# Two transformer blocks on one Trainium2 core: selected-keys attention on key partitions, and norms in two halves of tokens

## The reference

```python
# block 1
h = rms_norm(x, g_mix)
q, k, v, qi, ki, wi, conv_in, qc, gate_pre = split(h @ w_in)
y_att  = dsa_attention(rope(q), rope(k), v, rope(qi), rope(ki), wi) @ w_att_out
y_conv = (bg * causal_dwconv(cg * u)) @ w_conv_out
y_mem  = memory_attention(qc, rms_norm(mem, g_mem) @ w_mem_kv) @ w_mem_out
x = x + (sigmoid(gates) * [y_att, y_conv, y_mem]).sum() @ w_o
gate, val = split(causal_dwconv(rms_norm(x, g_ffn) @ w_up))
x = rms_norm(x + (silu(gate) * val) @ w_down, g_final)
# block 2: stick-breaking attention (12 heads) and memory attention (4 heads)
y = concat(stick_breaking(x @ w_in_sb), memory_attention_2(x, mem_2 @ w_mem_kv_2)) @ w_out
x = layer_norm(x + y)
x = layer_norm(x + square(relu(x @ w_up_2)) @ w_down_2)
# dsa_attention, for each block of 128 queries: 6 heads of 64, 2 groups of keys/values
score = sum_h(wi * relu(qi @ ki.T)), causal
sel = top_k(score, 256)
p = softmax(q @ k[sel].T / 8)      # three heads share a group's keys
o = p @ v[sel]
```

## Time and profile before

| | us |
|---|---|
| median of 3 runs (lowest to highest) | 3177.89 (3175.38 to 3183.56) |
| the profiled execution, its own time | 3180.83 |
| its span | 3179.0 |
| mean granted TensorE clock, share of full speed | 0.957 |

### The profile page before, as it was taken

How to read it: one execution, slowest core, us unless ns; L and a number is a source line. 1 busy time by engine, 2 the same in 40 slices (tenths; PEclk the granted TensorE clock), 3 DMA queues, 4 the chain that set the end, 5 groups by cost and what they waited for, 6 DMA issues and landing times.

```text
span 3179.0 us, 35178 instructions
## 1 busy us (share of the span) xinstructions
PE 2945.3 (93%) x13338; PEld 2381.2 (75%) x13338; DVE 1697.7 (53%) x2259; ACT 755.1 (24%) x1320; POOL 1168.0 (37%) x649
## 2 busy tenths in 40 slices
PE   5977999998999899999999779999888999999996
PEld 3765878885778688888888567887676888888885
DVE  4475899985562533232332547888937333333327
ACT  3154000003531211011111245666613000000002
POOL 2320334441024233433444414555532443334331
PEclk9978999996999899999999889999988999999998
DMA  3110112221031011111112110000020111111111
...
DMA packets 42300, 165.39 MB, mean 52 GB/s; under 512 B 4688, under 2 KB 5968, under 8 KB 40656
## 3 DMA queue, kind: packets, MB, share of 16 engines
q1 hardware_dynamic: 35568, 129.31, 12.1%
...
...
## 4 chain that ended last, share of the span: by engine, by line
PE 81%; DVE 10%; issue 5%; ACT 2%; POOL 1%; DVEq 1%; DMA 1%; ACTq 0%; SPq 0%; POOLq 0%
PE dense L457 22%; PE dense L458 21%; PE dense L461 21%; DVE stay L1654 2%; PE dense L799 2%; PE side L708 2%; PE dense L800 2%; PE dense L801 2%; PE dense L718 1%; PE dense L635 1%; PE side L837 1%; DVE a_lo L1319 1%; DVE T L1263 1%; ACT T L977 1%; PE side L497 1%
## 5 line engine op out<-in xcount | busy, mean ns | idle before, releaser
L366 POOL TENSOR_TENSOR w_hi<-raw,zero 128x1024 fp32r<-128x1024 f32 x210 | 404.6, 1926 | 1586.7 <-PE dense L461 1475.4
L457 PE MATMUL dense<-a_hi,w_hi 128*128 128x512 f32 x2192 | 864.9, 395 | 42.4 <-DVE a_lo L1319 20.0
L458 PE MATMUL dense<-a_lo,w_hi 128*128 128x512 f32 x2192 | 860.7, 393 | 0.0
L461 PE MATMUL dense<-a_hi,w_lo 128*128 128x512 f32 x2192 | 681.1, 392 | 0.0
L368 POOL TENSOR_TENSOR w_lo<-raw,w_hi 128x1024 fp32r<-128x1024 f32 x210 | 530.6, 2527 | 16.5
L457 PEld LDWEIGHTS dense<-a_hi,w_hi 128*128 128x128 f32 x2192 | 416.2, 190 | 140.2 <-issue 40.2
L458 PEld LDWEIGHTS dense<-a_lo,w_hi 128*128 128x128 f32 x2192 | 416.1, 190 | 87.6 <-issue 1.2
L461 PEld LDWEIGHTS dense<-a_hi,w_lo 128*128 128x128 f32 x2192 | 415.6, 190 | 87.9
L457 PE MATMUL dense<-b_hi,w_hi 128*128 128x512 f32 x864 | 338.8, 392 | 5.4 <-DVE T L1567 2.5
L458 PE MATMUL dense<-b_lo,w_hi 128*128 128x512 f32 x864 | 336.3, 389 | 0.0
L1547 DVE TENSOR_TENSOR x_res<-x_res,dense 128x1024 f32<-128x1024 f32 x104 | 126.9, 1220 | 332.8 <-PE dense L461 331.1
...
## 6 DMA issues: line engine op xcount, KB each, us to landing
...
x_in<-in_x_t SPq DMA_DIRECT2D x4, 1024.0 KB, 8.7
...
```

Of the source, the lines that this page charges most:

```text
L366: pool.tensor_tensor(w_hi[:, r % 2, :], raw[:, r, :], zero[:, 0:1].broadcast_to([P, D]), ALU.add).then_inc(weights_rounded, 1)
L457: pe.matmul(o, w_hi[:, slot, w], hi[:, k, x], start=b == 0, stop=False)
L458: pe.matmul(o, w_hi[:, slot, w], lo[:, k, x], start=False, stop=False)
L461: last = pe.matmul(o, w_lo[:, slot, w], hi[:, k, x], start=False, stop=stop)
```

## The change

**Attention.** Keys lie on partitions. A step is (block i, group g) with the group's three heads side by side (384 columns): 16 steps, and 72 pieces (step, block of 128 keys). A piece is four fp32r matmuls into one bank (keys by rounded queries, keys by the queries' rest, mask by three identities, a row of ones by the row of negative bounds), an exponential of 128x384 on ACT, and one fp32 matmul with `v_ones`: 64 columns of values and 64 of ones, so that the output has the row sums beside the values. The bound is the row's masked maximum of logits made in one fp32r matmul, still with queries on partitions (`bound_logits`), in 48 maxima on DVE as before; three one-row matmuls turn the negated bounds (`turn_bounds`) and ACT copies them. At a step's end DVE takes the reciprocal of the 64x384 row sums and multiplies. `k_stack` (key and its rest) and `v_ones` are made ahead of the convolution stage; per step ACT rounds the queries twice (64x384) and DVE takes the rests. POOL makes the mask in six pieces. The bounds of step s stand on PE between the pieces of steps s-2 and s-1.

**Norms.** The 1024 tokens go in two halves of 512. Norm 0 loads x by halves and sums its squares with 8 fp32 matmuls a half, without DVE additions. For norms 1 and 3 the last two tiles before are done by halves (`last_two`: half 0 of both, then half 1 with the sums and the spread of half 0 between), and the first two tiles behind likewise (`first_two`: half 0 of both, the second tile four slices behind, with the second half's sums ahead of slice 2 and its spread ahead of slice 6). Norm 4 has its last four down outputs by halves and 16 stores. KV2's four tiles move from before REST to behind the last down tile, and norm 2's sums and spreads stand between them. The two first `w_o` tiles lose their lag of four slices (`two_tiles` had the second tile four slices behind the first).

```diff
-T_KV2 = T_FF + FULL * FF_TILES
-T_REST = T_KV2 + 4
-T_MEM2 = T_REST + 2 * REST + KB // 2
+T_REST = T_FF + FULL * FF_TILES
+T_KV2 = T_REST + 2 * REST + KB // 2
+T_MEM2 = T_KV2 + 4
...
+DSA_LEAD, DSA_LAG = 3, 2
+
+
+def bound_at(s, j):
+
+    first, last = DSA_X0[s - 2] - 1, DSA_X0[s - 1] - 2
+    return first + (last - first) * j // (REP - 1)
...
+NORM_SPLIT = (None, 2, 0, 2, 4)
+
+
+def pieces(norm):
+
+    m = NORM_SPLIT[norm]
+    return [(k, None) for k in range(KB - m)] + [(k, h) for h in range(2) for k in range(KB - m, KB)]
...
+            for h in range(2):
+                for c in range(4):
+                    sp.dma_start(x_in[:, 2 * c:2 * c + 2, cols(h)], io["x_t"][:, 2 * c:2 * c + 2, cols(h)]
+                                 ).then_inc(x_loaded[h][c], 16)
+                sp.dma_start(raw[:, h, :], io["w_stream"][h]).then_inc(weights_loaded[h], 16)
...
+            pool.wait_ge(picked, 1)
+            for i in range(TOPK // P, TB):
+                sc = slice(score_at(i), score_at(i + 1))
+                pool.tensor_scalar(mask_r[:, sc], score[:, sc], TAKEN / 2, NEG, ALU.is_gt, ALU.mult).then_inc(masked, 1)
...
+            def first_two(t, u, ready, sums=None, spread=None, sums_at=2, spread_at=6, lag=4):
+
+                for n in range(KB + lag):
+                    if n == sums_at and sums is not None:
+                        sums()
+                    if n == spread_at and spread is not None:
+                        spread()
...
+            def square_sums(norm, h):
+
+                pe.wait_ge(added, added_before(norm, KB - 2, h) + 1)
+                sum_part(T[:, 3, :], cols(h), 0, True, False)
+                pe.wait_ge(squares, squares_before(norm, KB - 1, h) + 1)
+                sum_part(T[:, (KB - 1) % 2, :], cols(h), 0, False, True).then_inc(sum_ready, 1)
...
+            def last_two(norm, t, u, sums):
+
+                for m in range(2):
+                    pe.wait_ge(sums_free[(u + m) % 2], (u + m) // 2)
+                    pe.wait_ge(weights_split, t + m + 1)
+                    half_product(t + m, half_bank(norm, KB - 2 + m, 0), a_hi, a_lo, 0, 0, KB, KB).then_inc(half_tile, 1)
+                o = half_bank(norm, KB - 2, 1)
+                half_product(t, o, a_hi, a_lo, 1, 0, 3, KB)
+                sums(0)
+                half_product(t, o, a_hi, a_lo, 1, 3, KB, KB).then_inc(tile_done, 1)
+                spread(norm, 0)
+                half_product(t + 1, half_bank(norm, KB - 1, 1), a_hi, a_lo, 1, 0, KB, KB).then_inc(tile_done, 1)
...
+            def bound_logits(n):
+
+                s, j = n // REP, n % REP
+                i, g = DSA_PLAN[s]
+                pe.wait_ge(dup_split, s + 1)
                 if n >= 2:
-                    b = n - 2
-                    i = DSA_PLAN[b][0]
-                    pe.wait_ge(lg_tc, TB + b + 1)
...
+                o = att_logit_bank(x)
+                pe.matmul(o, k_stack[:, g, keys], qd_hi[:, s % 4, :, :], start=True, stop=False)
+                pe.matmul(o, k_stack[:, g, keys], qd_lo[:, s % 4, :, :], start=False, stop=False)
+                pe.matmul(o, mask_r[:, score_at(i) + kb * P:score_at(i) + kb * P + P], ident3[:, :, :], start=False, stop=False)
+                pe.matmul(o, one_row[:, :], bound_row[:, s % 2, :], start=False, stop=True).then_inc(d_logits, 1)
...
+                pe.matmul(att_out_bank(s), v_ones[g][:, kb, :], att_w[:, x % 4, :], start=kb == 0, stop=kb == i
+                          ).then_inc(d_out, 1)
...
+            for x in range(len(DSA_KEYS) + DSA_LAG):
+                if x < len(DSA_KEYS):
+                    att_logits(x)
+                if x + 1 in DSA_X0[DSA_LEAD - 1:DSA_STEPS - 1]:
+                    turn_bounds(DSA_X0.index(x + 1) + 1)
+                for n in BOUND_AT.get(x, ()):
+                    bound_logits(n)
+                if x >= DSA_LAG:
+                    att_values(x - DSA_LAG)
...
             for n in range(4):
+                if n == 1:
+                    for h in range(2):
+                        square_sums(2, h)
+                if n == 3:
+                    for h in range(2):
+                        spread(2, h)
                 tile(T_KV2 + n, U_KV2 + n, hi=m_hi, lo=m_lo, width=MEM, ready=parts["mem2"][1] if n == 0 else None)
...
+            for g in range(GROUPS):
+                act.activation(k_stack[group_rows(g), g, :], k_f[group_rows(g), :], ACT.Copy).then_inc(kv_round, 1)
+            for g in range(GROUPS):
+                act.activation(v_ones[g][:, :, 0:HD], v_f[:, :, HD * g:HD * g + HD], ACT.Copy)
+                act.activation(v_ones[g][:, :, HD:P], v_f[:, :, HD * g:HD * g + HD], ACT.Copy, bias=1.0, scale=0.0)
...
+                    act.activation(att_w[:, x % 4, :], att_logit_bank(x), ACT.Exp, scale=SCALE).then_inc(d_exp, 1)
...
-                dve.tensor_tensor_reduce(out=T[:, n % 2, 0:w], in0=side[:, n % 2, 0:w],
-                                         in1=score[:, score_at(i):score_at(i) + w], scale=1.0, scalar=TAKEN, op0=ALU.add,
-                                         op1=ALU.max, accum_out=row_max[:, e:e + 1])
-                dve.drain()
-                dve.tensor_scalar(neg_max[:, e:e + 1], row_max[:, e:e + 1], -SCALE, None, ALU.mult).then_inc(lg_max, 1)
-                dve.wait_ge(lg_exp, TB + n + 1)
-                dve.reciprocal(inv_sum[:, e:e + 1], row_sum[:, e:e + 1])
-                dve.drain()
-                dve.tensor_scalar(T[:, n % 2, 0:w], T[:, n % 2, 0:w], inv_sum[:, e:e + 1], None, ALU.mult
-                                  ).then_inc(lg_p, 1)
...
+                dve.tensor_tensor_reduce(out=masked_out[:, n % 2, 0:w], in0=side[:, n % 2, 0:w],
+                                         in1=mask_r[:, score_at(i):score_at(i) + w].bitcast(F32), scale=1.0, scalar=TAKEN, op0=ALU.add,
+                                         op1=ALU.max, accum_out=row_max[:, e:e + 1]).then_inc(d_max, 1)
+                if n % REP == REP - 1:
+                    e -= REP - 1
+                    dve.drain()
+                    if s >= 2:
+                        dve.wait_ge(d_row, s - 1)
+                    dve.tensor_scalar(neg_max[:, e:e + REP], row_max[:, e:e + REP], -1.0, None, ALU.mult).then_inc(d_neg, 1)
...
+                    dve.wait_ge(d_out, e + 1)
+                    dve.reciprocal(att_inv[:, s % 2, :], att_out_bank(s)[HD:P, :])
+                    dve.drain()
+                    dve.tensor_tensor(ya_f[group_rows(g), :, i * P:i * P + P],
+                                      att_out_bank(s)[0:HD, :].rearrange("p (j q) -> p j q", j=REP),
+                                      att_inv[:, s % 2, :].rearrange("p (j q) -> p j q", j=REP), ALU.mult).then_inc(d_copied, 1)
...
```

931 lines of the change are left out of this document (630 added, 301 removed).

## The result

The changed kernel takes 3188.58 us (median of 8 runs, 3181.84 to 3195.77) against 3178.71 (8 runs); the ratio is 1.0031, with a 95% interval of 1.0018 to 1.0044. It is slower by 0.3%, where 3114 was forecast with a range of 3082 to 3148. The profiled execution has a span of 3180.8 us. It took 3182.97, 5.6 under the median of its eight: three of them (3181.84 to 3183.31) have a mean granted clock of 0.962 to 0.964, the other five (3188.38 to 3195.77) of 0.958 to 0.961, so a difference of medians to the changed kernel and one of traces need not agree.

What follows compares the result with a forecast made beforehand. TensorE, busy 93% of the span, was taken as the bound, so gains come from its waits or less or cheaper work: 12 + 9 + 2 + 16.5 + 15 + 5.5 + 3 = 63 us off 3180.8, 3114 in medians, range 3082 to 3148.

Steps and rivals of the forecast that it cites:

- A piece is four fp32r matmuls at 0.23 us or less: Attention on PE: each of a piece's four 384-column fp32r matmuls costs 0.23 us or less, about 0.175 at full clock.
- That is 1.35 to 1.5 a piece: Attention on PE: four fp32r matmuls plus one fp32 PV take 1.35 to 1.5 us a piece, 97 to 108 in all.
- The uncovered tail: End of attention: the last reciprocal, product, rounding and POOL's low part stay uncovered, 5.7 us where 2.17 was.
- Rival C: Attention: low clock or DVE stays last, 0 to +15 us instead of -12; 3126 to 3141, typically 3136; chance 0.18.
- rival E: Attention: the reciprocal chains the stage, from about 9.5 us an instruction; slower, 3186 or more; chance 0.03.
- Rival D: Norms 0, 1, 3, 4: POOL meetings and doubled instructions leave 10 us gain instead of 34; 3138 to 3158; chance 0.08.
- the fixed part of the doubled instructions: Norms: fixed cost of doubled DVE instructions eats gain; a 512 operation costs 0.62 of pace, half of 1.16 is 0.58.
- Norm 0: Start of kernel: first product near 24.5 instead of 48.5, two tiles end near 63 instead of 72.4; -9 us (5 to 11).
- The merged tiles without lag: -2: First w_o tiles behind the attention: dropping the lag saves 2 us (0 to 3).
- Norm 1: Behind w_o: from tile 7's first half, end at 42 to 43.5 us instead of 59.6; -16.5 (13 to 20).
- I counted two: Two-input DVE operations meeting POOL cost 2.2 us each; one more in norms 0, 1, 3, attention each gives back 9.
- Norm 2, 3, 4: Later norms: norm 2 with KV2 takes 23 us, -15 (10 to 17); norm 3 -5.5 (3 to 9); norm 4 -3 (0 to 6).

Runs made afterwards that it cites:

- e1: Changed kernel with the attention of before put back, all else (halved norms) still changed: 3168.89 us, ratio 0.9969 to the kernel before.
- e2: Changed kernel with the bound added by a matmul over 128 rows, 127 of them zero, instead of one row: 3164.99 us, ratio 0.9954 to the kernel before.
- e13: Changed kernel with the bound's matmul over 64 rows, 63 of them zero, instead of one: 3181.06 us (one run).
- e14: Changed kernel with the bound's matmul over 32 rows instead of one: 3186.29 us (one run).
- e11: Changed kernel with 128-row bound matmul, w_o lag put back, second memory's low part moved behind the feed-forward groups, wide diagonals: 3133.55 us, ratio 0.9861 to kernel before.
- e10: Changed kernel with old attention, w_o lag put back, second memory's low part moved behind the feed-forward groups, wide diagonals: 3139.77 us, ratio 0.9879 to kernel before.
- e9: Changed kernel with a half's four diagonal blocks made by one 128x512 VectorE instruction, in all norms: 3172.94 us, ratio 0.9984 to the kernel before.
- e5: Changed kernel with the four-slice lag between the first two w_o tiles put back: 3177.12 us, ratio 0.9998 to the kernel before.

## Why the prediction was wrong

The forecast was a gain of 63 us, the result a loss of 10. By e1, which has the old attention, some 40 of these 73 us are the norms' (a gain of 10.7 where 51 were forecast, the 2 of the missing lag among them) and some 32 the attention's (20 more where 12 less were forecast). A failed step stands behind either.

**Attention, PE: the first failed step.** "A piece is four fp32r matmuls at 0.23 us or less" and "That is 1.35 to 1.5 a piece" took all four to cost the same. The fourth has one row, and costs 0.39 us more with what it does to its neighbours (e2, e13, e14): 28 us over 72 pieces, and 23 of time in e2. The forecast took the price of its 384-wide rows for any number of rows; a change of it was to be seen in the trace of before, at L708. The rest of the piece was right: 1.34 in e2. The forecast for the stage, 163 us from its beginning, was missed by 8 to 9 us in e2 and e11 (172.1 and 170.6).

**Attention, the rest.** The reciprocal was forecast at 2.5 and took 2.56; the estimate of 3.2 worked out from the Trainium skill (VectorE: DVE Perf Modes, "First, the fixed hardware budget") was too high here. The piece loop began 24.9 us after the last gate product, where 19 were told. The queries were split 14.6 after it, two of the eight splits 0.5 us late beside POOL's masks; the other 10.3 went into three rounds of bound logits, maxima and turns between PE, at clock 0.50, and DVE, of which the forecast had only DVE's nine maxima. Piece 20 began at 811, 3 us after the forecast's latest, though the stage had begun 8 early; the 52 pieces behind it took 106 us for 80 to 88 (89.5 in e11), of which 52 times 0.39, 20 us, are the one-row matmul. The uncovered tail was 5.05 for 5.7. Rival C had the direction and not the cause: PE had 0.50 to 0.75 in the first blocks, but from 790 on the clock was full and PE last, and the stage was 20 longer for C's 15 at most. Only rival E, at 0.03, had a slower kernel, and by another engine: a reciprocal of 9.5 us or more.

**Rival D** (0.08) told the norms: 0, 1, 3 and 4 with 10 us instead of 34, by meetings with POOL. With the pair without lag they gave 8.1 - 1.8 + 2.4 + 0.8, 9.5 us by the table. Its other ground, the fixed part of the doubled instructions, was not what ate them: with three edits that leave the halved scaling and low parts as they are, the same norms give 31 (e10).

**Norm 0** came within 2 us: two tiles were done at 65.2 for 63. The first product stood at 27.4 for 24.5, as one diagonal block took 2.37 us beside POOL (24.6 in e9).

**"The merged tiles without lag: -2"** had the wrong sign. Counted were the waits for merged slices that it would save; left out was what is late next: both tiles end together, so both buffers come free together, and the next two wait, for POOL's splits in the trace after. It costs 6 to 7 us (e5), a step mis-sized by 8 to 9.

**Norm 1: the second failed step.** From the end of tile 7's first half to the end of the first feed-forward pair the forecast was 42 to 43.5 and it took 44.8 (1043.3 to 1088.1). The step that failed was behind it: what DVE has in its queue next. The memory's eight subtractions were not in the sum, since in the trace of before they took 2.78 us beside an idle POOL. In the changed kernel POOL splits two tiles just then: 10.54, and PE waits 8.21.

**"I counted two" meetings with POOL** was the step that failed in all norms. The mechanism was named with its row, but only two-input operations were counted, and too few. The diagonals have one SBUF tensor, and wait as well (three of four in norm 2, two of four in norm 3). The Trainium skill (SBUF — State Buffer, "Who interferes with whom") has this case, a `tensor_scalar` in a 2-port mode; that these instructions ran in one no run shows. Summed over what DVE's instructions took above the shortest of their line and shape, 13.8 us are lost from 1030 to 1100 and 10.1 from 1800 to 1860; in the trace of before it is 0.1 and 0.6 from 1030 to 1084 and from 1800 to 1860.

**Norm 2, 3, 4.** With the diagonals wide, norm 2 with KV2 is 22.9 for 23, and norm 3 saves 4.8 for 5.5. Norm 4 gave 0.8 of 3 (1.0 in e10): its half products stretch the end of the feed-forward by 4.6 us, and what lies behind it shrinks by 5.4.

With the mendings, and the lag back, the halved norms give 38.7 us (e10), where 49 were forecast without the lag's 2. In e10's trace the stages give 8.5 (norm 0, forecast 9), 16.5 (norm 1, 16.5), 13.4 (KV2 and norm 2, 15), 4.8 (norm 3, 5.5) and 1.0 (norm 4, 3), less 1.3 in the attention, 1.6 in the output products and 1.0 between norm 2 and `w_out`. The sizes of the norms were thus near but for what met POOL, the lag and norm 4. The large errors all went the same way: each left out what another engine or a neighbouring instruction does.
